# S5 gate projection moved into the recurrence, responses carried to the Toeplitz operand through DRAM, four response-column buffers

## The chip, the cores and the metric

One core of a Trainium2 chip. The metric is the device time of one execution, in microseconds: for the kernel before 1853.6 us, the median of three runs (1850.58 to 1854.81).

## The reference, cut to what matters

A small network in fp32: 256 tokens of width 1024 and 256 context tokens pass an attention layer (MLA), then an S5 layer, then a block with pooling and spatial gating, cross-attention to a memory and a convolutional feed-forward part. The change touches only the S5 layer:

```python
u_l, g_l = jnp.split(h_lat @ w_in, 2, axis=-1)     # 2048 channels each
u_c, g_c = jnp.split(h_ctx @ w_in, 2, axis=-1)
y = d_skip * u_l                                   # 128 groups of 16 channels
for direction in range(2):                         # forward and backward in time
    # 64 complex states a group: x[t] = lam_bar * x[t-1] + b_bar @ u[t],  y[t] += real(c @ x[t])
    y = y + scan(u_c, then u_l)
ya, yb = split(gelu(y) @ w_glu + b_glu, 2)
out = ((ya * sigmoid(yb)) * silu(g_l)) @ w_out
```

The gate projection is `g_l = h_lat @ w_in[:, 2048:]`, 1024 by 2048. Nothing needs it before the product with silu(g) behind the GLU.

## The kernel before, in words

The engines run programs of their own (PE for matmuls, DVE, ACT and POOL for elementwise work, SP for most transfers), joined by semaphores; each engine runs its instructions in order. Weights pass through a ring of four slots of 1 MB (8 blocks of 128 rows by 256 columns); SP fills slot after slot in the order of a list (PHASES, L521), each load behind a wait for the use of the slot four units earlier (stream, L567).

The S5 layer has three stages on PE.

- s5_u (L1027 to L1056), 8 units: the u half of w_in, for all 512 tokens. ACT copies the results to token tiles (L1475), PE transposes them by chunks of 8 tokens (u_columns), DVE copies them to u5 (L2047).
- s5_g (L1057, by linear, L838), 8 units: the gate half, for the 256 latent tokens, in order of chunks. ACT writes silu of them to gl (L1485).
- The recurrence (L1124 to L1136), 16 blocks of 8 channel groups. A chunk is L5 = 8 tokens. For block b, responses(b) (L1060) makes the impulse responses within a chunk, 15 lags of 16 channels, from the diagonal-blocked B (bbd) and the response columns cp, and adds the D diagonal (d_block, L1074). ACT copies them to kf (kfs, L1521), and 16 transfers of 32 KB spread kf over the 128 partitions of the Toeplitz operand t0, each with another shift: eight from SP (spread, L654) and eight from POOL (L2397). inputs(b) (L1079, matmuls in L1091) takes the chunk inputs ub and the input operator bm to PSUM; DVE's scan(b) (L2054 to L2098) turns, scans over the chunks, and turns back to x5; outputs(b) (L1095) multiplies ub by t0 (L1102) and then x5 by cp (L1110); ACT copies the result to tokens (tokens, L1531), PE transposes it (back, L1121), ACT writes gelu of it to yt (L1537).

On PE the order is inputs(0), responses(0), responses(1), and then for each block inputs(b + 1), outputs(b), responses(b + 2), back(b). On ACT it is tokens(b), decays(b + 2) (L1494), u_block(b + 2) (L1498), kfs(b + 2), b_diagonal(b + 3) (L1508 to L1510), back(b). SP's order in the loop (L684 to L701) is:

```python
wait in_done >= 2 * (b + 1);   load_bm(b + 2)          # L686, L687; 1024 KB, s_b_powers
wait x5_set  >= 4 * (b + 1);   load_trig(b + 2)        # 512 KB, s_turns
wait bbd_set >= b + 3;         load_b(b + 4)           # 128 KB, s_b_and_c
wait y_done  >= b + 1;         load_cp(b + 3)          # 1024 KB, s_c_powers
wait kf_set  >= 4 * (b + 3);   spread(b + 2)           # L697, L698: 8 x 32 KB
```

bm, kf, trig5, bb, ub have two buffers, t0 three, cp three: xc and the ring's slots 0 and 1. The ring's slots 2 and 3 hold the first two units of the GLU weights meanwhile. bm and cp are made earlier by POOL, as tables of powers (L2318 to L2361), while the attention runs, and are stored to DRAM (s_b_powers, s_c_powers); POOL loads the rows for them with an outermost dimension of 8 on both sides, stepping by 0 in the source for the B rows (L2306):

```python
pool.dma_start(gen_b[d]..., spill_cols[b, :, w].unsqueeze(0).to_broadcast([L5, CH5, half]))
```

Behind the recurrence comes the GLU (L1151), 32 loads of weights with 32 matmul groups each, then s5_out.

## Time and profile before

| | |
|---|---|
| Median of three runs | 1853.6 us |
| The profiled execution, its own time | 1855.85 us |
| Its span | 1854.0 us |
| PE busy | 1646.7 us, 89% of the span |
| DVE, ACT, POOL busy | 634.2, 410.3, 658.0 us |
| Mean DMA rate, in packets of all queues | 172 GB/s |
| s5_u | 675 to 804 us |
| gate stage | 804 to 861 us |
| recurrence | 861 to 1053 us |
| GLU | 1053 to 1276 us |

How to read it: times are from the span's start. A row's line number is that of the instruction in the kernel, and that may be the line of a helper that many stages use, as L838. fp32 matmuls stand in the trace as two records each, so a gate tile of 8 matmuls has 16, and the 8 units of the gate stage 256. PEclk is the TensorE clock granted, as a share of the full one. "x64" counts instructions merged in a row.

### The profile page before, as it was taken

The numbers are of one execution on the slowest core, as the hardware profiler recorded it, in microseconds if no ns is written. First come the engines' busy times: TensorE is split into PE (matmuls) and PEld (weight loads), VectorE is DVE, ScalarE is ACT, GpSimd is POOL, SyncE is SP. The second block draws the span as 40 slices with busy tenths as digits, with TensorE's granted clock in tenths as the row PEclk, the third lists the DMA queues.
The fourth block names the chain that finished last, engine by engine and source line by source line (L and its number), as shares of the span: only waits on it lengthen the run. The fifth ranks groups of instructions, "written<-read, shape, count | busy, mean of one in ns | idle before, by whom it ended". The sixth has DMA issues, their size and how long they took to land.

```text
span 1854.0 us, 27226 instructions
## 1 busy us (share of the span) xinstructions
PE 1646.7 (89%) x10616; PEld 1232.9 (67%) x10616; DVE 634.2 (34%) x1225; ACT 410.3 (22%) x922; POOL 658.0 (35%) x678
## 2 busy tenths in 40 slices
PE   3889999999999859998666799999989998999997
PEld 3444455555544448887555688888878786888786
DVE  4772565556520152113676400001032113233301
ACT  1524233333300010013554300000021001244300
POOL 0025999999899999801333100000000000000000
PEclk9899999999999979999777799999999999999999
DMA  8859768878788867437989644443423341344441
GB/s 271 264 126 301 223 117 210 203 172 183 196 193 201 191 111 194 140 98 239 288 284 285 214 146 156 158 143 130 158 88 117 114 136 60 122 159 147 142 131 56
DMA packets 241230, 318.31 MB, mean 172 GB/s; under 512 B 32274, under 2 KB 211061, under 8 KB 236405
## 3 DMA queue, kind: packets, MB, share of 16 engines
q1 hardware_dynamic: 204736, 227.58, 38.7%
q0 software_dynamic: 33072, 80.79, 19.7%
q10 hardware_dynamic: 3333, 8.71, 1.2%
q8 instruction: 61, 1.00, 0.2%
q14 instruction: 28, 0.23, 0.0%
HBM read 258.28 MB, written 50.33 MB: 166 GB/s over the span
## 4 chain that ended last, share of the span: by engine, by line
PE 79%; DVE 8%; DMA 4%; ACT 3%; issue 3%; SPq 3%; DVEq 0%; ACTq 0%; PEldq 0%
PE bank L838 39%; PE bank L1151 12%; PE bank L1036 6%; DMA arena<-s_b_powers 2%; SPq L654 2%; PE bank L905 2%; PE bank L1091 2%; PE bank L1207 1%; PE bank L969 1%; PE bank L938 1%; PE bank L937 1%; PE bank L935 1%; PE bank L936 1%; PE bank L933 1%; PE bank L806 1%
## 5 line engine op out<-in xcount | busy, mean ns | idle before, releaser
L838 PE MATMUL bank<-ht,ring 128*128 128x256 f32 (+1 forms) x1664 | 422.9, 417 | 9.8 <-DVE ht L2145 9.0
L838 PEld LDWEIGHTS bank<-ht,ring 128*128 128x128 f32 x1664 | 320.6, 193 | 110.0 <-issue 70.7
L1151 PE MATMUL bank<-arena,ring 128*128 128x256 f32 x1024 | 223.1, 381 | 1.1 <-PEq L1142 1.1
L1151 PEld LDWEIGHTS bank<-arena,ring 128*128 128x128 f32 x1024 | 195.8, 191 | 28.1 <-issue 1.2
L838 PE MATMUL bank<-gate,ring 128*128 128x256 f32 (+1 forms) x640 | 194.9, 467 | 4.9 <-DVE gate L2198 3.4
L838 PEld LDWEIGHTS bank<-gate,ring 128*128 128x128 f32 x640 | 122.4, 192 | 76.8 <-issue 63.1
L1036 PE MATMUL bank<-ring,ht 128*128 128x256 f32 x512 | 115.7, 389 | 19.4 <-DVE ht L1793 19.4
L1036 PEld LDWEIGHTS bank<-ring,ht 128*128 128x128 f32 x512 | 99.8, 196 | 33.9 <-issue 19.8
L838 PE MATMUL bank<-arena,ring 128*128 128x256 f32 x480 | 107.9, 388 | 3.9 <-DVE arena L2260 3.9
L838 PEld LDWEIGHTS bank<-arena,ring 128*128 128x128 f32 x480 | 93.8, 196 | 17.8 <-DVE arena L2260 4.3
L2397 POOL DMA_DIRECT2D arena<-arena x128 | 64.7, 513 | 112.8 <-ACT arena L1521 110.9
L1091 PE MATMUL bank<-gate,arena 128*64 128x64 f32 x1024 | 54.5, 300 | 35.9 <-DMA arena<-s_b_powers 32.6
L1091 PEld LDWEIGHTS bank<-gate,arena 128*64 128x64 f32 x1024 | 51.9, 211 | 37.9 <-DMA arena<-s_b_powers 34.3
L2117 DVE SCALAR_TENSOR_TENSOR gate<-bank,col,gate 128x256 f32<-128x256 f32 x16 | 7.7, 480 | 198.1 <-ACT gate L1576 198.1
L1936 DVE TENSOR_SCALAR arena<-arena 128x256 f32<-128x256 f32 (+1 forms) x64 | 70.7, 1105 | 2.3
L1928 DVE TENSOR_REDUCE arena<-bank 128x1 f32<-128x256 f32 (+1 forms) x64 | 35.6, 557 | 87.2 <-PE bank L938 51.4
L2047 DVE COPY arena<-bank 64x256 f32 x64 | 27.0, 422 | 97.5 <-PE bank L1047 95.7
L1409 ACT ACTIVATE arena<-bank,arena 128x256 f32<-128x256 f32 (+1 forms) x64 | 37.2, 581 | 104.4 <-DVE arena L1929 104.3
L2253 DVE SCALAR_TENSOR_TENSOR arena<-arena,col 128x256 f32<-128x256 f32 x44 | 21.3, 484 | 94.9 <-ACTq L1667 93.1
L2206 DVE TENSOR_TENSOR xl<-bank,xl 128x256 f32<-128x256 f32 x24 | 9.1, 419 | 129.9 <-PE bank L838 129.9
L1531 ACT COPY arena<-bank 32x128 f32<-32x128 f32 x128 | 33.0, 258 | 87.4 <-PE bank L1110 84.6
L2067 DVE TENSOR_TENSOR ht<-bank,gate 128x512 f32<-128x512 f32 x16 | 11.1, 692 | 109.7 <-PE bank L1091 109.5
(362 smaller groups left out, 2347.1 us busy)
## 6 DMA issues: line engine op xcount, KB each, us to landing
ring<-in_s_w_glu SPq DMA_DIRECT2D x32, 1024.0 KB, 5.4
ring<-in_w_mod SPq DMA_DIRECT2D x24, 1024.0 KB, 8.6
ring<-in_w_up SPq DMA_DIRECT2D x22, 1024.0 KB, 5.1
arena<-s_b_rows POOLq DMA_DIRECT2D x32, 512.0 KB, 11.4
arena<-s_power_rows POOLq DMA_DIRECT2D x32, 512.0 KB, 11.5
s_b_powers<-arena POOLq DMA_DIRECT2D x32, 512.0 KB, 3.1
s_c_powers<-arena POOLq DMA_DIRECT2D x32, 512.0 KB, 5.4
ring<-in_s_w_in SPq DMA_DIRECT2D x16, 1024.0 KB, 5.8
```

The source lines that it names most:

```text
L654: sp.dma_start(t0[b % 3][s * CH5:(s + 1) * CH5, :, 0, :], kf[b % 2][0:CH5, :, lo:lo + P])\
L838: mm = pe.matmul(psum[2 * (u % 2) + m][:, 0:mv.free_size()], ring[:, sl, k, m * P:(m + 1) * P], mv, start=(kg == 0 and k == 0), stop=(kg = ...
L905: mm = pe.matmul(bank[:, :], att_uq[b][:, c, lo:hi], qn[:, c, :], start=(c == 0), stop=(c == 1))
L1036: mm = pe.matmul(psum[2 * (u % 2) + s4 // 2][:, s4 % 2 * S:(s4 % 2 + 1) * S], ht[:, k, s4 * P:(s4 + 1) * P], ring[:, sl, k, :], start=(k = ...
L1091: mm = pe.matmul(psum[4 + z][g * ST5:(g + 1) * ST5, (d * BLK + q) * NC5:(d * BLK + q + 1) * NC5], bm[b % 2][:, d, z, q, g * ST5:(g + 1) * ...
L1151: mm = pe.matmul(psum[4 * par + 2 * (s // 2) + m][:, 0:S], ring[:, sl, k, m * P:(m + 1) * P], yt[:, kg * 8 + k, :], start=(kg == 0 and k = ...
L1409: act.activation(prob[e][:, t, 0:w], psum[2 + t][:, 0:w], ACT.Exp, bias=sm[:, e, 1, t:t + 1], scale=SM_SCALE, accum_out=sm[:, e, 2, t:t + ...
L1531: act.copy(ytok[0:NCL, :, lo:lo + CH5], psum[6 + g][q * NCL:(q + 1) * NCL, 0:P].rearrange("p (s c) -> p s c", c=CH5)).then_inc(ytok_set, 1)
L1928: link(dve.tensor_reduce(sm[:, e, 0, t:t + 1], psum[2 + t][:, 0:w], AX.X, ALU.max))
L1936: ts(prob[e][:, t, 0:w], prob[e][:, t, 0:w], sm[:, e, 3, t:t + 1], None, ALU.mult).then_inc(prob_set, 1)
L2047: dve.tensor_copy(u5[h * 64:(h + 1) * 64, bass.ds(i * 8 + (8 * s + 4 * q), 4), g, :], src[g * 64:(g + 1) * 64, :, h, :]).then_inc(ut_free[ ...
L2397: pool.dma_start(t0[b % 3][s * CH5:(s + 1) * CH5, :, 1, :], kf[b % 2][CH5:2 * CH5, :, lo:lo + P])\
```

## The change

- The gate projection leaves its stage. It is 16 tiles of 128 gate channels, one a block: gate_rows(t) on PE, gate_copy(t) on ACT, without silu. Its weights pass through the ring's slots 2 and 3, a unit every two blocks (load_gate). The latent h is copied to xc (h_s5), since the loop's scan uses ht. One Silu over all of gl follows behind the loop, ahead of the GLU's product.
- The responses go from kf to t0 in one store to DRAM (s5_responses, 32 rows of 7.5 KB) and two loads of 256 KB, one for each half of the groups, all from POOL; SP has no part in it. For that kf and t0 are laid out by lag first, and the order of the tokens within a chunk is turned (hence the turned halves in u_rows and u5 and the turned powers).
- cp has four buffers: two in the arena, and the ring's slots 0 and 1. t0 has two instead of three.
- SP asks for the input operator as soon as its buffer is free, ahead of the other loads of the loop.
- The D diagonal of a block is made by POOL in the loop, not by DVE for all blocks at once.

```diff
-        t0 = [c2(BLK, 2, P) for _ in range(3)]
+        t0 = [c2(2, L5, BLK, CH5) for _ in range(2)]
-        kf = [c2(BLK, KW5) for _ in range(2)]
+        kf = [c2(2 * L5 - 1, BLK, CH5) for _ in range(2)]
+        cp_rows = [c2(NTAB) for _ in range(2)]
-              (xc[:, :, :].rearrange("p a b -> p (a b)"), ring[:, 0].rearrange("p k m -> p (k m)"),
-               ring[:, 1].rearrange("p k m -> p (k m)"))]
+              (*cp_rows, ring[:, 0].rearrange("p k m -> p (k m)"), ring[:, 1].rearrange("p k m -> p (k m)"))]
+        h_s5 = xc
...
@@ SP @@
-            stream("s5_g", w5[:, E_BR:2 * E_BR], 1, 8)
-            def spread(b):
-                for s in range(L5):
-                    lo = (L5 - 1 - s) * CH5
-                    sp.dma_start(t0[b % 3][s * CH5:(s + 1) * CH5, :, 0, :], kf[b % 2][0:CH5, :, lo:lo + P])\
-                        .then_inc(t0_in[b % 3], 16)
+            def load_gate(s):
+                n = ring_at["s5_g"] + s
+                src = rows8(w5, 0, E_BR + s * MT2) if s < 8 else rows8(wg, s % 2, 0)
+                sp.wait_ge(slot_done, n - 3 if s < 2 else n - 1)
+                sp.dma_start(ring[:, 2 + s % 2], src).then_inc(w_in_[n % NSLOT], 16)
...
-            load_cp(0)
+            for b in range(2):
+                load_cp(b)
             for s in range(2):
-                sp.wait_ge(slot_done, at + s - NSLOT + 1)
-                load((at + s) % NSLOT, rows8(wg, s % 2, s // 2 * E_BR))
-            sp.wait_ge(slot_done, ring_at["s5_g"] + 8)
-            for b in range(1, 3):
+                load_gate(s)
+            for b in range(2, 4):
+                sp.wait_ge(slot_done, ring_at["s5_u"] + 5 + b)
                 load_cp(b)
             for b in range(2):
                 sp.wait_ge(bbd_set, b + 1)
                 load_b(b + 2)
-            for b in range(2):
-                sp.wait_ge(kf_set, BLK * (b + 1))
-                spread(b)
+            sp.wait_ge(in_done, 2)
+            load_bm(2)
+            load_gate(2)
             for b in range(NB5):
+                if b + 3 < NB5:
+                    sp.wait_ge(in_done, 2 * (b + 2))
+                    load_bm(b + 3)
                 if b + 2 < NB5:
-                    sp.wait_ge(in_done, 2 * (b + 1))
-                    load_bm(b + 2)
                     sp.wait_ge(x5_set, 4 * (b + 1))
                     load_trig(b + 2)
                 if b + 4 < NB5:
                     sp.wait_ge(bbd_set, b + 3)
                     load_b(b + 4)
-                sp.wait_ge(y_done, b + 1)
-                if b + 3 < NB5:
-                    load_cp(b + 3)
-                if b + 2 < NB5:
-                    sp.wait_ge(kf_set, BLK * (b + 3))
-                    spread(b + 2)
-                if b >= NB5 - 3 and b % 3:
-                    s = 2 + (b % 3 - 1)
-                    load((at + s) % NSLOT, rows8(wg, s % 2, s // 2 * E_BR))
+                if b + 4 < NB5:
+                    sp.wait_ge(y_done, b + 1)
+                    load_cp(b + 4)
+                if b % 2 and b < 14:
+                    load_gate((b + 5) // 2)
+            for s in range(2, 4):
+                sp.wait_ge(y_done, NB5 + s - 3)
+                load((at + s) % NSLOT, rows8(wg, s % 2, s // 2 * E_BR))
@@ PE @@
-            linear("s5_g", 1, 8, lambda k: ht[:, k, :].rearrange("p (j c) -> p j c", c=NC5)[:, :, NCL:NC5])
+            def gate_rows(t):
+                s = t // 2
+                n = ring_at["s5_g"] + s
+                if t % 2 == 0:
+                    pe.wait_ge(w_in_[n % NSLOT], 16 * (n // NSLOT) + 16)
+                pe.wait_ge(gl_set, t + 1)
+                for k in range(KD):
+                    mm = pe.matmul(psum[2][:, 0:S], ring[:, 2 + s % 2, k, t % 2 * P:(t % 2 + 1) * P], h_s5[:, k, :],
+                                   start=(k == 0), stop=(k == KD - 1))
+                mm.then_inc(slot_done if t % 2 else gate_done, 1)
             def responses(b):
                 pe.wait_ge(bbd_set, b + 1)
+                pe.wait_ge(diag_set, b + 1)
...
             def outputs(b):
-                pe.wait_ge(t0_in[b % 3], 128 * (b // 3 + 1))
-                pe.wait_ge(t0_odd_in[b % 3], 128 * (b // 3 + 1))
+                pe.wait_ge(t0_in[b % 2], 32 * (b // 2 + 1))
...
+            gate_rows(0)
+            responses(0)
             inputs(0)
-            responses(0)
             responses(1)
+            gate_rows(1)
             for b in range(NB5):
                 if b + 1 < NB5:
                     inputs(b + 1)
                 outputs(b)
                 if b + 2 < NB5:
                     responses(b + 2)
+                    gate_rows(b + 2)
                 back(b)
@@ ACT @@
+            act.copy(h_s5[:, :, :].rearrange("p k (j c) -> p (k j) c", c=NCL),
+                     ht[:, :, :].rearrange("p k (j c) -> p (k j) c", c=NC5)[:, :, NCL:NC5]).then_inc(gl_set, 1)
...
+            def gate_copy(t):
+                if t % 2:
+                    act.wait_ge(slot_done, ring_at["s5_g"] + t // 2 + 1)
+                else:
+                    act.wait_ge(gate_done, t // 2 + 1)
+                act.copy(gl[:, t, :], psum[2][:, 0:S]).then_inc(gl_set, 1)
...
             def kfs(b):
                 act.wait_ge(kf_done, b + 1)
                 if b >= 2:
-                    act.wait_ge(t0_in[(b - 2) % 3], 128 * ((b - 2) // 3 + 1))
-                    act.wait_ge(t0_odd_in[(b - 2) % 3], 128 * ((b - 2) // 3 + 1))
+                    act.wait_ge(kf_stored[b % 2], 16 * (b // 2))
...
                 if b + 3 < NB5:
                     b_diagonal(b + 3)
+                if b + 2 < NB5:
+                    gate_copy(b + 2)
                 back(b)
+            act.wait_ge(gl_set, NB5 + 1)
+            act.activation(gl[:, :, :]..., gl[:, :, :]..., ACT.Silu).then_inc(gl_set, 1)
@@ POOL @@
+            def diagonal(b):
+                tt(d_block[b % 2][0:2 * CH5], ..., ALU.mult).then_inc(diag_set, 1)
...
             for b in range(NB5):
                 pool.wait_ge(kf_set, BLK * (b + 1))
-                if b >= 3:
-                    pool.wait_ge(y_done, b - 2)
-                for s in range(L5):
-                    lo = (L5 - 1 - s) * CH5
-                    pool.dma_start(t0[b % 3][s * CH5:(s + 1) * CH5, :, 1, :], kf[b % 2][CH5:2 * CH5, :, lo:lo + P])\
-                        .then_inc(t0_odd_in[b % 3], 16)
+                pool.dma_start(spill_k[b], kf[b % 2][0:2 * CH5].rearrange("p i q c -> p (i q c)")).then_inc(kf_stored[b % 2], 16)
+                if b + 2 < NB5:
+                    diagonal(b + 2)
+                if b >= 2:
+                    pool.wait_ge(y_done, b - 1)
+                pool.wait_ge(kf_stored[b % 2], 16 * (b // 2 + 1))
+                for g in range(2):
+                    rows = bass.AP(spill_k.tensor, (b * 2 + g) * CH5 * wide_k, [[BLK * CH5, L5], [wide_k, CH5], [1, BLK * P]])
+                    pool.dma_start(t0[b % 2][:, g].rearrange("p i q c -> p (i q c)"), rows).then_inc(t0_in[b % 2], 16)
```

## Rows read from the trace of the kernel before

**Rows 1.** The page, its first line.

```profile
span 1854.0 us, 27226 instructions
```

**Rows 2.** Windows: PE, PEld, DVE, ACT, POOL busy, PEclk, DMA share, GB/s.

```profile
803.00:861.00 58.00, 57.72 (x260) 50.17 (x260) 4.59 (x9) 7.27 (x17) 0.17 (x1) 0.97 0.55 189
872.00:1053.00 181.00, 117.65 (x2864) 100.15 (x2864) 122.79 (x247) 87.00 (x268) 61.24 (x122) 0.74 0.84 265
```

**Rows 3.** The chain of waits, 795 to 900 us: start, us, what.

```profile
803.70 57.08 PE bank L838 x256
...
878.93 0.59 SPq L654
879.57 5.10 DMA arena<-s_b_powers
```

**Rows 4.** Waits, 872 to 1053 us: us in total, times, longest.

```profile
PE bank L1091 <- DMA arena<-s_b_powers: 32.6, 13, 4.4
```

**Rows 5.** Timeline: last matmuls of outputs(0) and outputs(14); start, us.

```profile
875.70 1.92 PE L1110 MATMUL bank<-xc,arena 64*32 64x128 f32 x64
...
1039.22 1.35 PE L1110 MATMUL bank<-ring,arena 64*32 64x128 f32 x64
```

**Rows 6.** Timeline: PE's groups of one block; inputs(b) at both clocks.

```profile
863.45 2.08 PE L1091 MATMUL bank<-gate,arena 128*64 128x64 f32 x64 [2.68 <-ACT gate L1498]
...
907.44 3.68 PE L1091 MATMUL bank<-gate,arena 128*64 128x64 f32 x64 [2.78 <-DMA arena<-s_b_powers]
...
968.24 0.66 PE L1102 MATMUL bank<-arena,gate 128*32 128x128 f32 x16
...
968.83 1.16 PE L1110 MATMUL bank<-ring,arena 64*32 64x128 f32 x64
...
969.92 1.08 PE L1069 MATMUL bank<-ring,arena 128*32 128x128 f32 x32
...
970.93 0.25 PE L1074 MATMUL bank<-gate,cst 32*32 32x16 f32 x8
...
972.33 0.68 PE L1121 MATMUL bank<-cst,arena 32*128 32x32 f32 x8 [1.15 <-ACT arena L1531]
```

**Rows 7.** Timeline: end of POOL's tables, last transposed copies on DVE.

```profile
781.03 0.59 POOL L2353 DMA_DIRECT2D s_c_powers<-arena  x1 [0.30 <-POOL arena L2352]
...
799.39 7.22 DVE L2047 COPY arena<-bank 64x256 f32 x16 [11.09 <-PE bank L1047]
```

**Rows 8.** Timeline: ACT's work for a block, and one scan on DVE.

```profile
944.58 0.69 DVE L2067 TENSOR_TENSOR ht<-bank,gate 128x512 f32<-128x512 f32 x1 [2.97 <-PE bank L1091]
...
951.75 0.89 DVE L2098 TENSOR_TENSOR arena<-ht 128x128 f32<-128x128 f32 x4
...
970.04 2.24 ACT L1531 COPY arena<-bank 32x128 f32<-32x128 f32 x8 [2.90 <-PE bank L1110]
...
972.30 0.61 ACT L1494 COPY ht<-r 128x504 f32<-128x504 f32 x1
...
973.46 1.48 ACT L1521 COPY arena<-bank 32x240 f32<-32x240 f32 x4
```

**Rows 9.** Windows: columns as in rows 2.

```profile
838.00:852.00 14.00, 14.00 (x67) 12.32 (x66) 0.00 (x0) 2.60 (x5) 0.00 (x0) 1.00 1.04 400
895.00:918.00 23.00, 15.48 (x384) 13.44 (x384) 16.40 (x34) 11.40 (x36) 8.06 (x16) 0.75 0.95 305
```

**Rows 10.** Transfers, 600 to 760 us; then GB/s in 40 slices, 737 to 757.

```profile
s_b_powers<-arena POOLq DMA_DIRECT2D x9, 512.0 KB, 3.1
arena<-s_b_rows POOLq DMA_DIRECT2D x8, 512.0 KB, 11.6
...
s_c_powers<-arena POOLq DMA_DIRECT2D x8, 512.0 KB, 5.6
...
GB/s 147 180 365 389 383 397 375 420 377 279 221 139 246 221 172 221 205 156 132 123 41 156 434 401 90 0 0 0 0 0 0 0 0 0 0 0 0 0 0 141
```

**Rows 11.** Windows of 1 us: columns as in rows 2.

```profile
951.00:952.00 1.00, 0.00 (x0) 0.00 (x0) 1.00 (x5) 0.85 (x4) 0.73 (x2) 0.50 1.06 451
```

80 lines of the change are left out of this document (42 added, 38 removed).

## The prediction

> **What bounds the kernel now.** The span is 1854.0 us [rows 1]. The profiled execution took 1855.85 us, 1.85 more than its span and 2.25 more than the median 1853.6 of the three runs shown; the sum below is made against 1855.85 and then lowered by 2.25. I read the windows first: two stretches in a row are touched. In the gate stage (803 to 861 us) PE is busy 57.72 of 58 us at a clock of 0.97: PE alone sets it. In the recurrence (872 to 1053 us) PE is busy 117.65 of 181 us, so 63 us are idle, at a mean clock of 0.74; since there are two levels, 1.2 and 2.4 GHz, about half of that time was spent at the lower one. DMA is busy 0.84 of it and moves 265 GB/s [rows 2]. The chain of waits then shows who sets these stretches: the gate stage is one piece of PE of 57.08 us, and behind it come SP's issues of the Toeplitz copies (L654), then the load of the input operator that waited behind them in SP's queue, then PE [rows 3]. The waits give the price of that last link: PE's inputs(b) waited 32.6 us in 13 places for that load [rows 4]. The period of a block is read from the ends of outputs(0) and outputs(14): 875.70 + 1.92 = 877.62 and 1039.22 + 1.35 = 1040.57, so 162.95 / 14 = 11.64 us [rows 5].
>
> **Part 1, the gate stage.** Its 57.08 us go. Two of the sixteen gate tiles come ahead of the loop, between s5_u and outputs(0); a tile is 57.08 / 16 = 3.57 us [rows 3]. PE's groups at the full clock: inputs 2.08, outputs 0.66 + 1.16, responses 1.08 + 0.25, back 0.68 [rows 6]. From 803.7: gate tile, responses(0), inputs(0) end at 803.7 + 3.57 + 1.33 + 2.08 = 810.7; u_block has its input by then, since the last transposed copies end at 799.39 + 7.22 = 806.6 [rows 7]. The scan takes DVE from 944.58 to 952.64, 8.06 us [rows 8], so outputs(0) could end at 810.7 + 8.1 + 1.2 = 820. The responses are the later ones: behind the last transposed copies ACT has two u_blocks, a gate copy, two decays and a diagonal, some 4 us, then the response copies of 1.48 [rows 8], to about 812.3; then come a store, two loads (part 2) of about 3.8 and 5.9 us, and 1.8 us of outputs: 823.8, against 877.62 now. **Term 1: 54 us saved**, between 48 (the loads collide) and 57.6 (the scan is last). The collision: POOL's tables end with the issue at 781.03 [rows 7] and SP may then load two input operators, four response columns and two gate units, 8 x 1.05 MB = 8.4 MB; at 400 GB/s [rows 9] that is 21 us, to about 806 us, with only the last two, wanted later, behind 800 us. The copy of h into xc, the tables' order, the turned halves of tokens and the D diagonals on POOL (four ops on 32 partitions, in a queue that idles) I cost at nothing: s5_u is 14 us of PE work a unit and covers the copy; without that cover it would be some 2 us once. One Silu over all 4096 columns instead of 16 lies after the loop, beside the first GLU unit, 28 us long (4 loads of 223.1 / 32); it costs at most 6 us if that cover failed.
>
> **Part 2, the period of a block, P.** Four things must fit in it.
> - PE: 2.08 + 1.82 + 1.33 + 0.68 + 3.57 = 9.48 us [rows 3, 6], plus five changes of group at 0.1 to 0.2 us: **10.2**.
> - DMA: a block now moves 1.05 (input operator) + 1.05 (response columns) + 0.52 (turns) + 0.13 (B) + 0.52 MB (16 Toeplitz copies). After it moves 2.75 + 0.52 (half a gate unit) + 0.25 (store of the responses) + 0.52 (their load) = 4.04 MB. Large loads alone ran at 400 GB/s, while two whole blocks with their 32 KB copies ran at 305 GB/s and a share of 0.95 [rows 9]. So P is 10.1 at 400 and 13.2 at 305; as the small copies go, I take 370: **10.9**.
> - The trip through DRAM, two blocks long. From y_done(b-2): ACT's tokens 2.24, two copies of 0.61, response copies 1.48 [rows 8], with waits 5.2 us; POOL's issue 0.7; the store, by the nearest rows 3.1 to 5.6 us landed for 512 KB; two issues 1.3; two loads of 256 KB. Their nearest row is the load of the B rows, which has the same outer dimension of 8 and lands in 11.6 us where a store of its size lands in 3.1; the slices behind the SP load of that stretch show only 120 to 250 GB/s [rows 10]. So the loads are 4.6 us (0.52 MB at 200 GB/s and 2) to 11.6. The sum is 15 to 24.4, in the middle 19.5; with outputs' 1.8 us it goes round twice a period: P is 8.4 to 13.1, **10.7**.
> - DVE: 8.06 us [rows 8]. ACT: about 6.6 with the gate copy.
>
> SP's queue loses eight issues a block (5 to 6 us) and no longer waits for the response copies ahead of the next loads. Each has a buffer free one to two periods before its use, so the 32.6 us [rows 4] go. What SP now waits for: a gate unit's release by gate_rows in odd blocks, with only the next input operator behind it, not wanted for a whole period. Behind POOL's wait for the store stands only the D diagonal of a later block. On PE, back(b) and inputs(b+2) now stand behind the gate tile; the tile fills the 2.24 us in which back waited for ACT's tokens anyway. What is late next is the DMA, hardly behind it the trip through DRAM and PE. With four floors within 0.7 us and jitter between them I take **P = 11.0**, bounds 9.6 and 12.9. **Term 2: 14 x (11.64 - 11.0) = 9 us saved**, bounds +29 and -18. The last block and the GLU stay as they are.
>
> The Trainium skill has a rule against this edit ("DMA: Bandwidth & Descriptors", "Why a DMA increments its semaphore by 16 and not by 1"): a copy runs on the largest number of DMA engines up to 16 that divides the outermost dimension of both its patterns, so a load whose source starts with 8 would use 8 of the 16. The slow landing of the B rows agrees [rows 10]. By the rule the loads would stand at the upper end: the second rival.
>
> **The clock.** In the 1 us window at 951, PE has nothing to do and the clock stands at 0.50; inputs(b) behind such gaps takes 3.68 us, not 2.08 [rows 6, 11]. After the change PE is busy 9.5 of 11 us, in gaps of under 1 us, so I take the full clock for most of it; the 0.4 us between the largest floor and 11.0 holds a few dips.
>
> **Sum.** 54 + 9 = 63 us; 1855.85 - 63 = 1792.9, less 2.25 is **1790.6 us**.
>
> **The rivals.**
> - PE alone sets the pace (DMA as fast as 400 GB/s, the trip hidden): P = 9.6 to 10.2, term 2 is 20 to 29, time 1771 to 1780. For it: slices above 400 GB/s. Against: two other floors lie there too. Chance 0.15.
> - The two t0 loads are slow and the trip is the bound: at 11.6 us for them and the middle of the store the trip is 5.2 + 0.7 + 4.3 + 1.3 + 11.6 = 23.1, P = 12.4, term 2 is -11 and the time 1811. For it: the landing of loads of this form [rows 10]. Against: those carry twice the bytes. Chance 0.15. (By the rule of the Trainium skill named above, this is the case.)
> - The queues are full, or the gate tile lies wholly in the path: P = 4.04 / 0.305 = 13.2 or 11.64 + 3.57 - 32.6 / 14 = 12.9, term 2 is -22 to -18, time 1822 to 1818. Against: the small copies that made 305 GB/s go, and PE has the idle time. Chance 0.10.
> - Slower: the clock stays at the lower level. By the ratio of inputs(b), 3.68 / 2.08 = 1.77 [rows 6], PE's 9.48 us become 16.8, with the changes 17.5: P = 17.5, term 2 is -82, time 1882. It decides from P = 11.64 + 54 / 14 = 15.5. For it: half the stretch now is at that level. Against: that stretch has 63 us of idle PE [rows 2], which the tiles fill. The Trainium skill ("TensorE: Matmul & The Clock Gate", "HAM oscillation") describes this case, a loop whose waits for DMA lower the clock anew in each turn. Chance 0.04.
> - The change doesn't do what it says: the first block waits some 54 us for its loads, and the gate stage has only become a gap; time within 0.2% of now. Against: the tables are out 20 us before [rows 7]. Chance 0.01.
>
> **The numbers.** P near 11 has a chance of 0.55 and the range 1780 to 1803. The whole range reaches from PE's floor over the second rival to the edge of the third: 1770 to 1818. A measurement of this kernel can tell about 0.2%, 4 us, from no change. Faster has 0.15 + 0.55 + 0.15 + 0.10 = 0.95, within 0.2% 0.01, slower 0.04.
>
> **What would show it.** In the profile after: no PE group of 57 us between s5_u and inputs(0); outputs(0) ending at 822 to 826; a period near 11.0; waits of L1091 for the input operator near zero; DMA over 350 GB/s and a share above 0.9 in the loop; a clock above 0.9. A wait of the first outputs matmuls for the t0 loads means the trip; a wait of the responses or inputs for the s_c_powers or s_b_powers loads means the DMA; no waits and a clock near 0.5 means the slower rival. The prediction is wrong if P is outside 9.6 to 12.9 or outputs(0) ends after 830.

## The result, and the profile after

The changed kernel takes **1820.55 us** (median of 4 runs, 1816.69 to 1822.22) against 1853.96 us for the kernel before, measured beside it (4 runs): a ratio of 0.9815 with an interval of 0.980 to 0.983. It is faster by about 33 us, 1.85%; the prediction had 63 and a range that ended at 1818.

The profiled execution after is the one of 1816.69 us, so against the profiled one of before (1855.85) it is 39.2 us shorter, which is what the steps below have to add up to. The page's first line and its part on the chain that ended last (shares of the span by engine, then by line):

```profile
span 1814.7 us, 26957 instructions
...
PE 77%; DMA 9%; DVE 6%; ACT 4%; issue 3%; SPq 1%; POOL 0%; DVEq 0%; ACTq 0%; POOLq 0%; PEldq 0%
PE bank L842 36%; PE bank L1168 12%; PE bank L1040 6%; DMA arena<-s_responses 4%; DMA s_responses<-arena 2%; PE bank L909 2%; PE bank L1224 2%; PE bank L973 1%; PE bank L942 1%; PE bank L941 1%; PE bank L939 1%; PE bank L940 1%; PE bank L937 1%; PE bank L810 1%; PE bank L936 1%
```

The 57 us of the gate stage are gone. Now 6% of the chain, over 100 us, is the trip of the responses: `s_responses<-arena` is the store to DRAM, `arena<-s_responses` the load of the Toeplitz operand. The timeline of PE gives the ends of outputs(0) and outputs(14), as in [rows 5] (start, us):

```profile
801.51 3.69 PE L1070 MATMUL bank<-xc,ring 128*128 128x256 f32 x16
...
825.39 1.10 PE L1116 MATMUL bank<-arena,gate 128*32 128x128 f32 x16 [10.13 <-DMA arena<-s_responses]
826.43 1.96 PE L1124 MATMUL bank<-arena 64*32 64x128 f32 x64
...
851.14 1.96 PE L1124 MATMUL bank<-ring,arena 64*32 64x128 f32 x64
...
996.90 1.16 PE L1124 MATMUL bank<-ring,arena 64*32 64x128 f32 x64
1000.39 1.06 PE L1135 MATMUL bank<-cst,arena 32*128 32x32 f32 x8 [2.33 <-ACT arena L1549]
1006.65 1.11 PE L1116 MATMUL bank<-arena,gate 128*32 128x128 f32 x16 [5.20 <-DMA arena<-s_responses]
...
1014.14 16.08 PE L1168 MATMUL bank<-arena,ring 128*128 128x256 f32 x66 [1.05 <-PEq L1159]
```

The first GLU matmuls in the kernel before:

```profile
1053.11 37.22 PE L1151 MATMUL bank<-arena,ring 128*128 128x256 f32 x163 [1.05 <-PEq L1142]
```

- outputs(0) ends at 828.39 instead of 877.62: **49.2 us saved**. (2.2 of them can't be put down to the change: the first gate tile starts at 801.51, and the gate stage of before at 803.70. In the profiles below of kernels made from the changed one this start lies anywhere from 801.2 to 806.5.)
- outputs(14) ends at 998.06, so the period is (998.06 - 828.39) / 14 = **12.12 us**, longer than the 11.64 of before: 14 x 0.48 = **6.7 us lost**.
- From outputs(14) to the first GLU matmuls 16.08 us pass, against 12.54 before (1053.11 - 1040.57): **3.5 us lost**, in the last block, whose outputs wait 5.20 us for the Toeplitz load.
- Together 49.2 - 6.7 - 3.5 = 39.0.

What a block waits for is in the chain of waits, from the first store of responses to the third block's outputs (start, us, what):

```profile
809.61 4.43 DMA s_responses<-arena
814.05 0.29 issue
814.34 0.65 POOL arena L2433
814.99 10.36 DMA arena<-s_responses
825.39 1.10 PE bank L1116 x16
826.50 1.97 PE bank L1124 x64
829.34 0.26 ACT arena L1549
...
833.02 0.36 ACT arena L1538
833.38 0.28 issue
833.66 2.16 DMA s_responses<-arena
835.86 1.86 issue
837.72 0.62 POOL arena L2433
838.34 11.72 DMA arena<-s_responses
850.10 1.10 PE bank L1116 x16
```

One turn of that trip, from the end of outputs(0) to the end of outputs(2), takes 828.39 to 853.1, 24.7 us for two blocks. Two windows (the stretch of the old gate stage, then outputs(0) to outputs(14); columns as in [rows 2]), the waits from 800 to 1020 us, and the transfers from 828 to 998 us (count, size, median us from issue to landing):

```profile
803.00:861.00 58.00, 43.15 (x859) 35.97 (x857) 33.66 (x68) 26.36 (x73) 10.23 (x18) 0.88 0.86 268
828.39:998.06 169.67, 142.30 (x2912) 117.16 (x2912) 106.33 (x211) 84.51 (x251) 27.47 (x52) 0.92 0.94 294
```

```profile
PE bank L1116 <- DMA arena<-s_responses: 40.8, 13, 10.1
DVE ht L2091 <- DMA gate<-s_turns: 16.1, 4, 7.6
```

```profile
DMA packets 18359, 49.88 MB, mean 293 GB/s; under 512 B 3240, under 2 KB 11604, under 8 KB 15259
...
arena<-s_responses POOLq DMA_DIRECT2D x26, 256.0 KB, 9.4
...
s_responses<-arena POOLq DMA_DIRECT2D x14, 120.0 KB, 5.9
```

No wait for the input operator is left, where there were 32.6 us [rows 4]. In its place PE waits 40.8 us for the Toeplitz loads, 10.1 of them ahead of outputs(0). The granted clock is 0.92 of the full one, where it was 0.74 [rows 2]: the gate tiles did fill PE. But the DMA engines are busy 0.94 of the time and move only 294 GB/s; a block carries 49.88 / 14 = 3.56 MB. Two suspects stand side by side: the length of the trip (its loads land in 9.4 us), and the throughput of the DMA engines, by which everything, the trip's own transfers included, gets slower.

### The profile page after: what moved, and what is told of

Its sections match the earlier page's. It is cut to its first block, busy times and chain, and to the rows that moved or that the text cites. A ratio compares the mean times of both kernels' runs of the same rounds, so it can differ in the third digit from the quotient of the medians.

```text
span 1814.7 us, 26957 instructions
## 1 busy us (share of the span) xinstructions
PE 1628.8 (90%) x10616; PEld 1212.6 (67%) x10616; DVE 634.1 (35%) x1224; ACT 411.8 (23%) x907; POOL 626.4 (35%) x614
## 4 chain that ended last, share of the span: by engine, by line
PE 77%; DMA 9%; DVE 6%; ACT 4%; issue 3%; SPq 1%; POOL 0%; DVEq 0%; ACTq 0%; POOLq 0%; PEldq 0%
PE bank L842 36%; PE bank L1168 12%; PE bank L1040 6%; DMA arena<-s_responses 4%; DMA s_responses<-arena 2%; PE bank L909 2%; PE bank L1224 2%; PE bank L973 1%; PE bank L942 1%; PE bank L941 1%; PE bank L939 1%; PE bank L940 1%; PE bank L937 1%; PE bank L810 1%; PE bank L936 1%
## 5 line engine op out<-in xcount | busy, mean ns | idle before, releaser
L842 PE MATMUL bank<-ht,ring 128*128 128x256 f32 (+1 forms) x1408 | 364.8, 422 | 9.8 <-DVE ht L2168 9.0
L842 PEld LDWEIGHTS bank<-ht,ring 128*128 128x128 f32 x1408 | 270.4, 192 | 102.3 <-issue 70.1
L1040 PEld LDWEIGHTS bank<-ring,ht 128*128 128x128 f32 x512 | 98.3, 193 | 32.6 <-issue 18.9
L1070 PE MATMUL bank<-xc,ring 128*128 128x256 f32 x256 | 61.7, 395 | 0.0
L1070 PEld LDWEIGHTS bank<-xc,ring 128*128 128x128 f32 x256 | 48.9, 196 | 7.0 <-issue 0.2
L2433 POOL DMA_DIRECT2D arena<-s_responses x32 | 19.4, 609 | 91.4 <-DMA s_responses<-arena 88.2
L1116 PE MATMUL bank<-arena,gate 128*32 128x128 f32 x256 | 12.5, 315 | 40.8 <-DMA arena<-s_responses 40.8
## 6 DMA issues: line engine op xcount, KB each, us to landing
arena<-s_b_rows POOLq DMA_DIRECT2D x32, 512.0 KB, 11.4
arena<-s_power_rows POOLq DMA_DIRECT2D x32, 512.0 KB, 11.6
```

What stands on the lines that cost most here:

```text
L842: mm = pe.matmul(psum[2 * (u % 2) + m][:, 0:mv.free_size()], ring[:, sl, k, m * P:(m + 1) * P], mv, start=(kg == 0 and k == 0), stop=(kg = ...
L1040: mm = pe.matmul(psum[2 * (u % 2) + 1 - s4 // 2][:, (1 - s4 % 2) * S:(2 - s4 % 2) * S], ht[:, k, s4 * P:(s4 + 1) * P], ring[:, sl, k, :], ...
L1070: mm = pe.matmul(psum[2][:, 0:S], ring[:, 2 + s % 2, k, t % 2 * P:(t % 2 + 1) * P], h_s5[:, k, :], start=(k == 0), stop=(k == KD - 1))
```

## The experiments

P is the period of a block, from the ends of outputs(0) and outputs(14) as above, read from the one profile of each kernel. Ratios are to the kernel before, measured beside each group of runs (1854.70, 1854.63, 1852.65, 1854.15, 1854.78 and 1851.62 us in the order in which they come). The expectations use four names. Theory A: the trip of the responses through DRAM sets the period. Theory B: the throughput of the DMA engines does. Theory C: the two bounds lie side by side, and later, for kernels without the trip, the DMA engines' throughput alone. Theory D: PE with its stalls.

Two cautions. Four executions of the changed kernel lie 5.5 us apart, so a difference in P of 0.2 or 0.3 us from one profile (3 or 4 us in 14 blocks) shows little by itself. And with the responses ahead of outputs the stretch that P is read from holds the responses of 13 blocks and not of 14, 1.33 us less of PE's work, up to 0.1 us a block.

### Each suspect by itself

**Responses early.** On PE, responses(b+2) goes ahead of outputs(b); on ACT its copies go ahead of tokens(b). The trip then starts before outputs(b) instead of behind it.

```diff
                 if b + 1 < NB5:
                     inputs(b + 1)
-                outputs(b)
                 if b + 2 < NB5:
                     responses(b + 2)
+                outputs(b)
+                if b + 2 < NB5:
                     gate_rows(b + 2)
```

> The changed kernel with responses(b + 2) ahead of outputs(b) on PE and the copies of the responses ahead of tokens(b) on ACT. The store then starts before outputs(b) ends, and only the two loads of t0 wait for it. Theory A, the trip of the responses through DRAM sets the period (12.12 us in the changed kernel): the round becomes about 0.1 + 1.3 + 9.4 + 1.8 = 12.6 us for two periods, which leaves the floors of PE (10.2) and of the transfers; period 10.5 to 11.2, time about 1820.6 - 14 x 1.3 = 1802. Theory B, the transfers' throughput sets it (share 0.94 busy at 294 GB/s): period stays at 11.9 to 12.3 and the time at 1817 to 1823.

Measured: 1814.05 us, ratio 0.9769 (0.9747 to 0.9791), P 11.70. PE's waits for the Toeplitz loads fall from 13 (40.8 us) to 5 (18.4 us), but the period follows only by 0.42 us, and the share of the DMA engines goes to 0.97 at 306 GB/s. Both the period and the time lie between what theories A and B expected. The trip was in the path; what stands behind it is near.

**Other order in DRAM.** The DRAM side of the Toeplitz loads starts with a dimension of 16 instead of 8 (so the operand's rows are exchanged); the bytes are the same.

```diff
-                    rows = bass.AP(..., [[BLK * CH5, L5], [wide_k, CH5], [1, BLK * P]])
+                    rows = bass.AP(..., [[wide_k, CH5], [BLK * CH5, L5], [1, BLK * P]])
```

> The changed kernel with the two dimensions of the DRAM side of the t0 loads exchanged, so that the outermost has 16 rows and not 8. The rows reach t0 in another order, so the Toeplitz part of the S5 output is computed from exchanged rows; bytes, packets and all waits are the same. Theory A with slow loads because of their form: the landing of the loads falls from 9.4 to 5 to 6 us, the period by half of it to about 10.5 to 10.9 and the time to about 1800. Theory A with loads slow only because the queues are full, and theory B: landing stays at 8.5 to 10 us, time 1816 to 1824. The rule of the Trainium skill (DMA: Bandwidth & Descriptors, Why a DMA increments its semaphore by 16 and not by 1) would have the loads run on 16 DMA engines and not 8.

Measured: 1807.99 us, ratio 0.9747 (0.9724 to 0.9771), P 11.52. The transfers from 828 to 990 us:

```profile
DMA packets 16688, 49.85 MB, mean 308 GB/s; under 512 B 1520, under 2 KB 9955, under 8 KB 13588
...
arena<-s_responses POOLq DMA_DIRECT2D x26, 256.0 KB, 7.9
```

The same 50 MB go in 1671 packets fewer, and the packets under 512 bytes are 1720 fewer, so the saving is all in the small ones. The load lands 1.5 us sooner, in 7.9 us, between the two ranges that were expected. 12 us of the time hang on the order in which one pattern is written, in a kernel whose Toeplitz operand has its rows exchanged and so doesn't compute the reference.

**Less to load.** 128 KB instead of 1024 KB for the gate units 2 to 7 (so most of the gate isn't the reference's), PE's work unchanged.

```diff
+                k8 = 1 if 2 <= s < 8 else 8
-                sp.dma_start(ring[:, 2 + s % 2], src)
+                sp.dma_start(ring[:, 2 + s % 2, 0:k8], src)
```

> The changed kernel with 128 KB instead of 1024 KB loaded for gate units 2 to 7, so that 12 of the 16 gate tiles use old weights in seven of their eight row blocks. Takes 6 x 0.92 MB off the loop of about 57 MB and changes no wait. Theory B: the period falls by 0.46 / 4.04 of 12.1, to about 10.8, time about 1803. Theory A: only the landings get a little shorter, period 11.6 to 12.0, time 1812 to 1820.

Measured: 1819.19 us in one run, P 11.88, DMA share 0.88. The time lies within the scatter of the changed kernel (1816.69 to 1822.22), so less traffic alone shows no gain: the trip holds the period, as theory A had it.

**No trip through DRAM.** The store and the two loads become sixteen copies of 32 KB on POOL's queue, from the response copies straight into the operand.

```diff
-                pool.dma_start(spill_k[b], kf[b % 2][0:2 * CH5]...)
-                pool.wait_ge(kf_stored[b % 2], ...)
-                for g in range(2):
-                    pool.dma_start(t0[b % 2][:, g]..., rows)
+                for s in range(L5):
+                    for g in range(2):
+                        pool.dma_start(t0[b % 2][s * CH5:(s + 1) * CH5, g]..., kf[b % 2][g * CH5:(g + 1) * CH5, s:s + L5]...)
```

> The changed kernel with the trip through DRAM undone: 16 transfers of 32 KB a block from kf to t0, all from POOL, in 2 KB pieces, and no store. Theory A: POOL issues for 16 x 0.51 = 8.2 us and the last lands some 2 to 5 us later, so the way from the response copies to t0 is 10.5 to 13.5 us against the changed kernel's 0.6 + 5.9 + 1.3 + 9.4 = 17.2; period 10.3 to 11 and time about 1800 to 1806. Theory B: the small transfers hold the DMA engines as before, period 12 or more, time 1820 to 1830.

Measured: 1816.41 us, ratio 0.9787 (0.9767 to 0.9807), P 11.92, DMA share 0.98 at 289 GB/s, neither theory's range. The interval overlaps that of the change itself: the trip through DRAM shows no gain over small copies from POOL's queue alone. The steps above put the gain where the gate stage was; how much of it each of the other edits carries (four response-column buffers, the order of SP's loads) was not tried by itself.

### Both, and who is not to blame

**Responses early and less to load**, the edits of the first and third run together.

> Both edits at once: responses ahead of outputs, and 128 KB instead of 1024 KB for gate units 2 to 7 (12 of the 16 gate tiles then use old weights in seven of eight row blocks). Alone the first left the period at 11.70 us with the transfers busy 0.97 of it, the second at 11.88 with 0.88 busy. Theory C, two bounds lie side by side, the trip at about 12 and the transfers at 3.56 MB / 306 GB/s = 11.6 us, and each edit lifts one only: together the period falls to 10.5 to 11.0. Theory A or B alone, or a third bound near 11.7 (PE, the scans): it stays at 11.5 to 11.8.

Measured: 1804.22 us in one run, P 11.15, DMA share 0.93. Alone they gave 6.5 us and 1.4, which is no more than scatter, together 16.3 (in P 0.42, 0.24 and 0.97 us a block): two bounds side by side. The period stays above theory C's range of 10.5 to 11.0.

**Turns early.** As the first run, and SP asks for the turns ahead of the input operator, since DVE had waited 26.5 us for them there.

```diff
-                if b + 3 < NB5:
-                    sp.wait_ge(in_done, 2 * (b + 2))
-                    load_bm(b + 3)
                 if b + 2 < NB5:
                     sp.wait_ge(x5_set, 4 * (b + 1))
                     load_trig(b + 2)
+                if b + 3 < NB5:
+                    sp.wait_ge(in_done, 2 * (b + 2))
+                    load_bm(b + 3)
```

> Responses ahead of outputs, and SP asks for the turns of block b + 2 as soon as scan(b) is done, ahead of the wait for inputs(b + 1) and the input operator. In the run with the first edit alone DVE waited 26.5 us in 7 places for the turns. If these waits lie on the path of the period, they go and the period falls by up to 1 us, to 10.8 to 11.3, time 1800 to 1806. By theory B (the transfers' throughput) the bytes stay and so does the period, 11.5 to 11.8, time 1811 to 1816.

Measured: 1810.28 us, ratio 0.9764 (0.9743 to 0.9785), P 11.66. DVE's waits for the turns are gone, the period is not shorter (11.70 before, 11.66 now), as theory B had it: with the DMA engines at 0.97, one load is only served before another. This is the fastest version that computes all of the reference; its interval overlaps that of the first run and lies below that of the change.

**One matmul of eight in the gate tile** of the changed kernel (so the gate isn't the reference's), with all loads.

```diff
-                for k in range(KD):
+                for k in range(1):
```

> The changed kernel with one of the eight matmuls of each gate tile, so that seven eighths of the gate projection are left out; all transfers and waits stay. PE's block gets 3.1 us shorter. If PE's work, or the gate tile's place ahead of back(b), is part of the period of 12.12, it falls to 11.0 to 11.6; by theories A, B and C it falls by at most 0.3, to 11.8 or more, since PE only waits longer for the t0 loads.

Measured: 1818.33 us in one run, P 12.09 with a clock of 0.79 in the loop. PE's busy time in the 14 blocks falls from 142.3 to 106.7 us and the period stays: PE's work is not what sets it in the changed kernel, and the gate tiles are free there.

**The order alone, in the kernel before.** SP asks for the input operator of b+3 before it waits with the Toeplitz copies of b+2. This takes the 32.6 us of [rows 4] away and nothing else of the change is there.

```diff
+                if b + 3 < NB5:
+                    sp.wait_ge(in_done, 2 * (b + 2))
+                    load_bm(b + 3)
```

> The kernel before with the one change that SP asks for the input operator of block b + 3 as soon as inputs(b + 1) is done, ahead of the spreads. PE's waits for that load (32.6 us in 13 places) should go. If they were worth their length, the period falls from 11.64 to about 9.5 to 10 and the time by 20 to 30 us, to 1825 to 1835. If the transfers' throughput (276 GB/s, busy 0.87, at 3.2 MB a block) is close behind, at 3.2 / 306 = 10.5, it falls to 10.6 to 11, the time by 9 to 15 us, to 1840 to 1846.

Measured: 1852.93 us, ratio 0.9987 (0.9977 to 0.9997), P 11.57. PE's waits (877 to 1053 us) show why:

```profile
PE bank L1073 <- DMA ring<-s_c_powers: 22.6, 7, 6.7
PE bank L1073 <- DMA xc<-s_c_powers: 16.6, 5, 6.4
```

PE waits 39.2 us for the response columns, where it had waited 4.8 us for them in the kernel before; the waits for the input operator are gone. The time is outside both ranges that were expected, 1825 to 1835 and 1840 to 1846. A wait for one load that is taken away came back as a wait for another.

### Towards a better version

**Eight loads instead of two**, on the version with responses and turns early: one for each step s, of 64 KB, outermost dimension 16, every row in its place.

```diff
-                for g in range(2):
-                    pool.dma_start(t0[b % 2][:, g]..., rows)
+                for s in range(L5):
+                    rows = bass.AP(..., [[wide_k, CH5], [CH5 * wide_k, 2], [1, BLK * P]])
+                    pool.dma_start(t0[b % 2][s * CH5:(s + 1) * CH5]..., rows)
```

> The whole computation. As the run with responses and turns early (period 11.66, 1810.28 us, DMA share 0.97 at 307 GB/s), but each pair of t0 loads (2 x 256 KB, outermost dimension 8) becomes eight loads of 64 KB with an outermost dimension of 16, the same bytes at the same places. Theory C (the DMA engines' time is the bound that is left once the trip has been put ahead): the form of the loads cost engine time there, so their queue's share falls by 3 points as in the run with exchanged rows, the period falls to 11.2 to 11.5 and the time to 1802 to 1808; POOL's six more issues a block (some 4 us) fit into its idle queue. Rival 1 (the form is not what costs, only the bytes do): period 11.6 to 11.8, time 1809 to 1813. Rival 2 (the issues on POOL lengthen the trip by 4 us and the trip decides): period 12.5 or more, time above 1818.

Measured: 1822.31 us, ratio 0.9821 (0.9780 to 0.9862), P 12.46. PE's waits for the Toeplitz loads are 23.8 us in 9 places (11.4 in 5 without the edit). That is rival 2, but for 0.04 us of its period: six more issues on POOL at about 0.65 us are 4 us on the trip, by the sum; the issues alone, without the other form of the loads, were not tried.

**Responses early and the other order in DRAM**, on the version with the turns early too (the Toeplitz operand's rows exchanged).

> The Toeplitz operand's rows are exchanged, so the outputs of the recurrence are not the reference's; all instructions and bytes are as many as in the run with responses and turns early. Only the order of the DRAM side of the t0 loads differs: outermost 16 instead of 8, still two loads of 256 KB. Theory C: both bounds are lifted at once here (the trip is ahead, the loads use less engine time and land some 1.5 us sooner), so the period is 11.2 to 11.4 and the time 1800 to 1806, below both the run with the order alone (11.66, 1810.28) and the run with exchanged rows alone (11.52, 1807.99). Rival (exchanging the rows had shortened the trip and nothing else, so that on top of the order it adds nothing): 11.6 to 11.7 and 1808 to 1812.

Measured: **1797.63 us**, ratio 0.9694 (0.9654 to 0.9733), P 11.16, better than theory C's own range. The gains add up: 10.3 us for the order of the work (1820.55 to 1810.28), 12.6 for the pattern (to 1807.99), 22.9 for both (to 1797.63).

**The same with every row in its place**: u, the input operator and the Toeplitz operand all in the row order (half, column, step).

```diff
-    utok = [... "p (g s c) -> p g s c" ...]
+    utok = [... "p (g c s) -> p g s c" ...]
+                for h in range(2):
+                    rows = bass.AP(spill_bm.tensor, ..., [[NTAB, CH5], [CH5 * NTAB, 4], [1, NTAB]])
+                    sp.dma_start(bm[b % 2][h * 64:(h + 1) * 64]..., rows)
```

> The whole computation, as the run with responses and turns early (period 11.66, 1810.28 us), but the rows of the recurrence's operands are put in the order (half, column, step) on every side (u by the copy and the transposes, the input operator by its load, the Toeplitz operand by its load), so that every t0 load has an outermost dimension of 16. The cost: the t0 operand comes by four loads of 128 KB instead of two of 256 KB (1.3 us more of issues on POOL ahead of the last), the input operator by two loads of 512 KB, and the copies of u write with a stride of 16 bytes. Theory C: the form gives what it gave in the run with exchanged rows (period 11.16, 1797.63), less some 0.3 us a block for the longer trip (six more issues cost 0.8 us a block in the run with eight loads): period 11.3 to 11.6, time 1799 to 1806. Rival (the length of the trip decides alone, and issues cost it as much as the form gives): period 11.6 to 12.0, time 1808 to 1814.

Measured: 1823.96 us, ratio 0.9843 (0.9814 to 0.9872), P 12.31: outside both ranges. PE waited for the Toeplitz loads only 8.5 us; the transfers (833 to 1006 us) show the engines full at a lower rate, with the landings of all large loads up (the input operator, now in two pieces, 11.1 us; response columns 12.9 and 14.5):

```profile
DMA packets 17484, 50.14 MB, mean 290 GB/s; under 512 B 2181, under 2 KB 10722, under 8 KB 14383
...
arena<-s_b_powers SPq DMA_DIRECT2D x24, 512.0 KB, 11.1
arena<-s_responses POOLq DMA_DIRECT2D x57, 128.0 KB, 7.4
arena<-s_c_powers SPq DMA_DIRECT2D x6, 1024.0 KB, 12.9
ring<-s_c_powers SPq DMA_DIRECT2D x6, 1024.0 KB, 14.5
```

That the input operator's gathered rows cost this was not tried by itself. So the gain of the run before is shown for the transfers, and no version here has it with all rows in place: of the two that tried, one took 1822.31 us and the other 1823.96.

### Is the rest the DMA engines or PE?

**The trip taken out.** The Toeplitz loads read rows that lay in DRAM long before, in the same pattern, as soon as the buffer is free; the store stays, and nobody waits for it before the last block (so the operand doesn't hold the responses).

```diff
-                pool.wait_ge(kf_stored[b % 2], 16 * (b // 2 + 1))
-                    rows = bass.AP(spill_k.tensor, ...)
+                    rows = bass.AP(spill_bm.tensor, ...)
```

> From the changed kernel. The two t0 loads of a block read rows that have lain in DRAM since the tables (s_b_powers), in the same pattern and as many bytes, and are asked for as soon as their buffer is free; the store of the responses stays but nobody waits for it. So the Toeplitz operand does not hold the responses and the outputs are not the reference's; instructions and bytes are as before, only the trip is gone. Theory C (two bounds side by side, the trip at about 12.1 and the DMA engines at 11.3 to 11.4 us of their time a block): the period falls from 12.12 only to 11.4 to 11.7, the DMA share is 0.97 or more, and outputs(0) ends 8 to 10 us earlier, near 819 (the scan or DMA then sets it): 1801 to 1806 us. Rival 1 (the trip was the only bound, and DMA or PE follow near 10.9, as the prediction had it): period 10.8 to 11.2, time 1793 to 1799. Rival 2 (the trip was never in the path, the waits for it only stood in for others): period 12.0 to 12.2, time 1810 or more.

Measured: 1809.23 us, ratio 0.9742 (0.9715 to 0.9768). outputs(0) ends at 820.3, 8 us sooner, as expected of theory C; but P is 12.56, above every range. outputs(14) ends at 996.1, only 2 us before the changed kernel's. What is loaded in the whole stretch is a reading that explains the two together: outputs(0) no longer waits until the backlog of first loads is through, so that the loop carries it. The windows from 785 us, the tables' end, to the end of outputs(14), first the changed kernel, then this one:

```profile
785.00:998.06 213.06, 172.83 (x3302) 142.81 (x3301) 130.33 (x262) 93.51 (x273) 39.23 (x66) 0.91 0.93 297
```

```profile
785.00:996.13 211.13, 179.54 (x3314) 146.83 (x3312) 132.57 (x267) 94.49 (x274) 44.56 (x69) 0.91 0.98 305
```

63.2 and 64.4 MB: the same load, at 297 and 305 GB/s, and without the trip the engines are busy 0.98 of these 211 us. In this profile PE stalls 27.9 us in ten places inside groups of matmuls that have no wait before them, with its work of 148.0 us all of the 175.8 us; one of them (start, us; what stands in brackets is the idle time before; the other 7 records of the group end at 844.95):

```profile
849.64 1.70 PE L1084 MATMUL bank<-arena 128*32 128x128 f32 x25 [4.69 <-issue]
```

So either the DMA engines set the end, or PE with these stalls. Two more kernels part them.

**The same with one matmul of eight in the gate tile:** PE's work taken away, the transfers left.

> As the run without the trip (period 12.56, 1809.23 us; PE 148.0 us busy and 27.9 us in stalls that no wait explains, of 175.8), but the gate tile has one matmul of eight, so the gate is not the reference's either; PE has some 3.1 us less work a block, DMA traffic is the same. Theory D (PE with its stalls is the bound there): the period falls by 1 to 3 us until the DMA engines' time stops it, to 11.2 to 11.6, time 1794 to 1802. Theory C (the DMA engines' throughput from the tables' end on is the bound, whatever PE does): the period stays within 0.4 us of 12.56 and the time within 4 us of 1809; PE then waits for loads instead of stalling.

Measured: 1806.65 us, ratio 0.9751 (0.9734 to 0.9767), P 12.18. The window from outputs(0) to outputs(14):

```profile
820.77:991.34 170.57, 123.92 (x2716) 98.60 (x2716) 114.14 (x226) 84.03 (x251) 34.62 (x54) 0.76 1.00 308
```

PE has 24 us less work and the time moves by 2.6 us, with ratios whose intervals overlap: theory C. The DMA engines are busy all of the time at 308 GB/s, and DVE waits 53.7 us for the turns instead of 15.0. So PE was not the bound in the run before either, though its work and stalls filled the time there.

**The same as the run without the trip, with less DMA time:** 128 KB for gate units 2 to 7, and the outermost 16.

> As the run without the trip, but with less DMA time: 128 KB instead of 1024 KB for gate units 2 to 7 and the t0 loads with outermost 16 (neither Toeplitz operand nor gate as in the reference); PE's work is the same. Engine time saved, by the runs that had one of the two each: 0.95 and 0.65 us a block. Both theories expect a gain here; they differ in the stalls. Theory D (the stalls are PE lacking instructions while the DMA engines are full): with a share below 0.93 the stalls fall from 27.9 us to under 10 us in the 14 blocks, the period to 10.6 to 11.0, 1786 to 1793 us. Theory C (the stalls are a by-product, throughput decides): share stays at 0.97 or more, the stalls stay near 20 us, the period is 11.0 to 11.4, 1791 to 1797 us. If the period stays above 12, neither DMA time nor the trip is the bound and something on PE itself is.

Measured: 1787.36 us, ratio 0.9644 (0.9627 to 0.9660), P 10.90:

```profile
819.53:972.13 152.60, 137.82 (x2912) 113.54 (x2912) 113.32 (x226) 84.61 (x251) 32.24 (x54) 0.94 0.91 307
```

137.8 us of work and 14.8 us of stalls are all of the 152.6 us again, but now the DMA engines have 0.09 to spare, so here PE with its stalls is probably the bound; less work on PE was not tried on this kernel. The period and the time are in theory D's ranges; the stalls, halved, are between the two theories. What the two runs show together: 24 us less of PE's work gave 2.6 us, and 6 MB less to load (58.3 instead of 64.4) with the cheaper form of the loads gave 22. Only with both of these and no trip does the loop get the 11.0 that was predicted for the change itself.

**What the stalls are.** This can be read from the traces that are there. Besides the data, the DMA engines carry a queue of kind instruction, q8, with packets of 16 KB. In the 175.8 us of the run without the trip it has 23 packets and PE 2912 matmul records, one packet to 126.6 records. The first line is that window's, the second that of 847.00 to 849.64, within the stall shown above:

```profile
q8 instruction: 23, 0.38, 0.9%
q8 instruction: 1, 0.02, 2.5%
```

The one packet inside the stall starts at 847.10 and takes 1.07 us; PE goes on at 849.64, 1.5 us after it is through. The ten stalls of this run all end 1.2 to 1.5 us behind such a packet. Of all 98 stalls over 0.6 us in the 14 blocks of the sixteen profiles, 97 end 1.2 to 1.7 us behind one, and in the run without the trip they are about 126, 253 or 380 matmul records apart, so that each falls where one packet's worth of records ends. The reading that fits both is that PE had run out of instructions and the next packet of them came late. What made it late isn't shown: the stalls are 9.9 to 27.9 us where the DMA share is 0.97 or more, and 0 to 16.3 us at 0.87 to 0.94.

## Why the prediction was wrong

The step that failed is the period of a block: its DMA floor and its trip floor were both sized too small, and two floors so near each other were taken to cost 0.1 us more than the larger. That is 15.7 of the 24 us between the 63 predicted and the 39.0 of the profiles.

- **The gate stage** (term 1, 54 us): 49.2 measured, inside its bounds of 48 and 57.6. PE and the scan came as worked out, inputs(1) ends at 815.3, and in the run without the trip outputs(0) does end at 820.3, the 820 that the step gave for the scan. The response copies were even done at 809.3, 3.0 us before the 812.3 of the sum. What was mis-sized is the trip behind them: 4.4 us for the store and 10.4 for the loads instead of 3.8 and 5.9, 0.9 us of issue between them that the sum left out, and 3.0 us for outputs instead of 1.8. The collision was seen, and its price taken too low.
- **The period** (term 2) is the step that failed: 11.0 us taken, 12.12 measured, so +9 became -6.7 us. Two of its floors were wrong.
  - *DMA, 10.9.* The bytes were too many (4.04 MB; 3.56 measured: the store's 32 rows have 3.75 KB and not the 7.5 of the section on the change, so 0.12 MB and not 0.25, and some first loads lie ahead of the loop). The rate was far too high: 370 GB/s taken "as the small copies go", 294 measured, and 301 to 308 with the engines at 0.97 to 1.00 and the loads in this form. The two errors partly cancelled: the right bytes at 370 GB/s would have been 9.6 us. The row of 305 GB/s at a share of 0.95 [rows 9] was the right one, and 370 was a choice between it and a stretch of large plain loads. 3.56 MB at 306 GB/s are 11.6 us, and the runs with the trip put ahead stop close to it (11.70, 11.66). That it is the engines that stop them is argued from the share of 0.97 and from the turns that moved and gained nothing; less work on PE was not tried there, and PE's work of 141.2 us and its stalls of 16.3 fill most of the 163.7 us of the first of them.
  - *The trip, 10.7.* Taken at 19.5 us and outputs' 1.8, measured at 24.7 for the turn shown and 24.2 in the mean (twice 12.12). In the middle its store lands in 5.9 us and its loads in 9.4, where the step had 4.3 and 8.1, the means of its bounds. With the measured landings its own sum is 5.2 + 0.7 + 5.9 + 1.3 + 9.4 + 1.8 = 24.3 us and P = 12.15: the mechanism was right and these two terms too small. The store came out above the largest of its rows (5.6), the loads between the mean and the upper end of 11.6 [rows 10].
  - *PE, 10.2,* was right for its work (142.3 / 14 = 10.16 us), and less work on PE alone gives nothing (12.09). PE's stalls were not foreseen; in the run in which both other bounds are eased they are 1.05 of the 10.90 us. DVE's 7.6 us a block (106.3 / 14) are below its 8.06.
- **Floors within 0.7 us** (the prediction says four; by its own numbers it is three, 10.2, 10.7 and 10.9, since DVE's 8.06 is not near) were combined by adding 0.1 us to the largest. Two of them aren't independent: the trip is made of transfers, and busy engines lengthen it. With the trip put ahead the period is 11.70, with less traffic 11.88, with both 11.15.
- **The last block** was costed at nothing and lost 3.5 us: its outputs wait 5.20 us for the same loads.
- **The rivals.** Nearest was the second, slow Toeplitz loads, with P = 12.4 and 1811 us: its period was right within 0.3 us, its time missed the start's and the last block's 8 us. It held the trip to be the only bound, though, and the DMA engines stand right behind it. The Trainium skill's rule ("DMA: Bandwidth & Descriptors", "Why a DMA increments its semaphore by 16 and not by 1") stood behind it. With a source that starts with 16 the load lands in 7.9 instead of 9.4 us and the kernel is 12 us faster, so the trace agrees in direction; how many engines a load used was not read, and the fall in packets under 512 bytes is a second explanation that no run parts from it. Of the third rival, the full queues are close to what happened (a share of 0.94, though 3.56 MB and not 4.04 to move) and the gate tile in the path is excluded by the one-matmul run. The lower clock is excluded by the 0.92.
- **The signs.** The wait of the first outputs matmuls for the Toeplitz loads was named as the sign of the trip, and it is PE's longest wait. The rate of over 350 GB/s, named as a sign of being right, was 294. Neither sign of being wrong came (P outside 9.6 to 12.9, outputs(0) after 830: they are 12.12 and 828.39), and still the time is outside the range, because the start, the period and the last block all came out on the slow side.

Summed: 54 became 49.2, 9 became -6.7 and nothing became -3.5, so 63 became 39.0. The medians differ by 33.4, because the profiled execution of before lay 1.9 us above the median of 1853.96 and the one of after 3.9 below its own.

## What to carry to other kernels

When a stage is folded into a loop to fill an idle engine, count the bytes that the loop moves and cost them at the rate of the busiest mixed stretch in the trace (here 305 GB/s), not at that of large plain loads (400). Cost a dependent round trip through DRAM at the landing times of such a stretch. In a loop whose DMA engines were some 0.9 busy or more, a wait for one load that was taken away brought nothing in either of the two runs that tried it: look first for bytes and packets to save, and for a chain's start that can be moved ahead of the work which doesn't need it. The order of the dimensions in a pattern is worth a try, since it gave 12 us for one line; but here that line left the rows exchanged, and both versions with every row in place lost the gain again.

## What the runs showed that was not expected

- A load of 256 KB of 2 KB rows takes 9.4 us to land with its DRAM side as 8 x 16 rows and 7.9 as 16 x 8, with 3240 and 1520 packets under 512 bytes in the loop.
- The DMA engines are full (share 0.97) at 307 GB/s with responses and turns early, and at 322 GB/s when only the pattern of the Toeplitz loads is turned; with the operands' loads cut and gathered otherwise they are at 0.98 with 290 GB/s. The GB/s alone don't tell that they are full.
- PE stalls inside groups of matmuls without any wait, up to 4.69 us at a time: 27.9 us in 14 blocks without the trip, 25.0 with the gate's matmuls taken away as well, 16.3 with the responses early, 14.9 in the kernel before with the other order, 1.9 in the changed kernel and none in the run with less to load and nothing else. They end right behind the arrival of a 16 KB packet on an instruction queue, 97 of 98 of them; why the packets are late stays open.
